# Filter norms as columns of 128 channels, spread by TensorE, and the filter spectra one turn later

## What is computed

```python
def hyena_filters(...):                       # weights only, no tokens
    h = (hid @ w3).reshape(L, ORDER, 2, D) * exp(-t * abs(deltas))
    h_fwd, h_bwd = h[:, :, 0], h[:, :, 1]
    two_sided = concatenate([h_fwd[:1] + h_bwd[:1], h_fwd[1:], zeros, flip(h_bwd[1:])])
    two_sided = two_sided * rsqrt(sum(square(two_sided), axis=0) + 1e-6)   # one norm per order and channel
    return rfft(two_sided, n=2 * L, axis=0)

def peer_ffn(h, ...):                         # 8 heads x 16 chosen experts for each token
    act = gelu(einsum('td,thkd->thk', t, u_tab[idx]))
    return einsum('thk,thkd->td', gate * act, v_tab[idx])
```

## Time and profile before

| | us |
|---|---|
| median of 3 runs | 1937.98 (1936.33 to 1944.38) |
| the profiled execution's own time | 1935.79 |
| its span in the trace | 1934.0 |
| TensorE matmul busy | 1690.3 (87%) |
| VectorE busy | 1500.2 (78%) |
| ScalarE busy | 593.4 (31%) |
| bytes moved | 665.11 MB, mean 344 GB/s |

### The profile page before, as it was taken

The page is one execution under the profiler, slowest core; times in us unless marked ns, Lnnn a source line. Parts: engine busy times, 40 slices in busy tenths (PEclk is TensorE's granted clock), DMA queues, the critical chain, the costliest instruction groups (busy, mean ns, idle before and its releaser), DMA issues.

```text
span 1934.0 us, 18185 instructions
## 1 busy us (share of the span) xinstructions
PE 1690.3 (87%) x5422; PEld 934.6 (48%) x5422; DVE 1500.2 (78%) x3548; ACT 593.4 (31%) x1427; POOL 483.3 (25%) x516
## 2 busy tenths in 40 slices
PE   5999999997999877899898999879989987877776
PEld 5778468653554432343343677545444433332232
DVE  6899996766778767888886699787678778777755
ACT  2555672312222323323242121023222232322221
POOL 0000000022334333343333100023333333333331
PEclk9999999998999998998999999889999999999999
DMA  8333118978999999999999775679999999999996
GB/s 348 120 120 113 50 58 316 387 276 347 364 427 419 426 408 406 380 418 413 425 414 426 312 302 201 245 294 415 427 426 426 421 425 414 417 426 420 426 417 280
DMA packets 95170, 665.11 MB, mean 344 GB/s; under 512 B 11323, under 2 KB 13020, under 8 KB 15456
## 3 DMA queue, kind: packets, MB, share of 16 engines
q0 software_dynamic: 73728, 536.90, 67.3%
q1 hardware_dynamic: 21344, 127.05, 17.0%
HBM read 662.79 MB, written 1.11 MB: 343 GB/s over the span
## 4 chain that ended last, share of the span: by engine, by line
PE 47%; DMA 24%; DVE 20%; issue 4%; ACT 2%; PEld 1%; DVEq 0%; PEldq 0%; POOL 0%; SPq 0%; POOLq 0%; ACTq 0%
DMA expert_rows<-in_p_uv,chosen_experts 23%; PE bank L1056 23%; DVE dot_products L2222 4%; PE bank L1032 4%; PE bank L818 3%; PE bank L862 3%; PE bank L934 2%; DVE conv_work_or_state L1860 2%; DVE silu_c_row_and_products L1668 2%; PE bank L878 1%; PE bank L889 1%; PE bank L1248 1%; PE bank L1092 1%; ACT weight_diagonal L1517 1%; PE bank L1175 1%
## 5 line engine op out<-in xcount | busy, mean ns | idle before, releaser
L1056 PE MATMUL bank<-expert_rows,weight_diagonal 128*128 128x512 f32 x2048 | 967.8, 617 | 173.5 <-ACT weight_diagonal L1517 172.8
L1288 POOL DMA_INDIRECT expert_rows<-in_p_uv,chosen_experts x512 | 483.1, 944 | 1424.3 <-PE bank L1056 795.1
L2222 DVE SCALAR_TENSOR_TENSOR dot_products<-expert_rows,bank 128x1024 f32<-128x1024 f32 x512 | 624.9, 1220 | 255.6 <-DMA expert_rows<-in_p_uv,chosen_experts 241.6
L1056 PEld LDWEIGHTS bank<-expert_rows,weight_diagonal 128*128 128x128 f32 x2048 | 385.2, 196 | 689.1 <-issue 398.0
L1517 ACT ACTIVATE weight_diagonal<-constants,expert_weights 128x128 f32<-128x128 f32 x512 | 177.8, 394 | 243.8 <-DVE expert_weights L2154 235.3
L1509 ACT ACTIVATE expert_gelu<-expert_dots 128x2 f32<-128x2 f32 x258 | 52.3, 203 | 627.4 <-DVE dot_products L2222 627.0
L818 PE MATMUL bank<-mixer_input_T_hi,weights_hi 128*128 128x512 f32 (+1 forms) x192 | 74.8, 389 | 22.0 <-DVE mixer_input_T_lo L1752 14.7
L1860 DVE SCALAR_TENSOR_TENSOR conv_work_or_state<-conv_work_or_state,channel_vectors 128x252 f32<-128x252 f32 (+1 forms) x192 | 82.5, 431 | 4.9 <-ACT conv_work_or_state L1371 0.4
L1175 PE MATMUL bank<-hyena_input_T,hyena_weight_block 128*128 128x256 f32 x320 | 71.1, 380 | 4.3 <-DMA hyena_weight_block<-in_h_in_blocks 4.3
L818 PE MATMUL bank<-mixer_input_T_lo,weights_hi 128*128 128x512 f32 (+1 forms) x192 | 72.4, 377 | 0.0
L818 PE MATMUL bank<-mixer_input_T_hi,weights_lo 128*128 128x512 f32 (+1 forms) x192 | 72.4, 377 | 0.0
(11 more groups left out here) (298 smaller groups left out, 1935.8 us busy)
## 6 DMA issues: line engine op xcount, KB each, us to landing
weight_block<-in_ada_rows SPq DMA_DIRECT2D x24, 1024.0 KB, 7.0
weight_block<-in_m_in_blocks SPq DMA_DIRECT2D x20, 1024.0 KB, 4.9
hyena_weight_block<-in_ada_rows SPq DMA_DIRECT2D x16, 1024.0 KB, 5.4
hyena_weight_block<-in_h_in_blocks SPq DMA_DIRECT2D x12, 1024.0 KB, 7.3
weight_block<-in_wq_blocks SPq DMA_DIRECT2D x11, 1024.0 KB, 7.6
expert_rows<-in_p_uv,chosen_experts POOLq DMA_INDIRECT x512
out_weights<-in_m_out_blocks SPq DMA_DIRECT2D x6, 1024.0 KB, 9.5
hyena_weight_block<-in_h_out_blocks SPq DMA_DIRECT2D x4, 1024.0 KB, 7.2
```

The costliest lines, as they stand in the source:

```text
L1056: last = mm(ps[b][:, :], dg[n % DIAG][:, :], uv[slot][:, D + h * 512:D + (h + 1) * 512], start=(r == 0 and k == 0), stop=end)
L1288: pool.indirect_dma_start(uv[slot][:, :], None, A[f"p_uv{l}"], bass.IndirectOffsetOnAxis(ap=chosen[:, s_, k:k + 1], axis=0)).then_inc(uv_l ...
L2222: stt(prod[:, :], uv[slot][:, 0:D], 1.0, rows_t, ALU.mult, ALU.mult, accum_out=dots[:, s_, k + j:k + j + 1]).then_inc(sem("dots_done"), 1)
```

## The change

The squares become the stationary operand and one column of the constants the moving one, so that the sum of a channel lands once, on the partition of that channel: 4 columns of 128 channels. Epsilon, root and reciprocal are taken on those 128x4 values. ScalarE then makes four diagonal matrices of them (`norm_diagonals`), TensorE multiplies these with a matrix of ones (`hrows`), which spreads the norms over all partitions again, and ScalarE copies the result to SBUF (`norm_rows`). In the second step the calls move: epsilon from k = 0 to k = 2, the root from 0 to 2, the reciprocal from 2 and 4 to 4, `hrows` stands at k = 7, the blocks of the spectrum go from k = 1, 3, 7, 9, 11 to 1, 8, 9, 11, 13, and their products from k = 6, 8, 10, 12, 14 to 8, 10, 12, 14, 14.

```diff
+    rsn_column = small[:, 1, 18:22]
+    rsn_diagonals = kT[:, 0:4, :]
...
                 plan.use(("hnorm", m), 4)
+                plan.use(("hrows", m), 4)
...
                     b = begin(("hnorm", m))
-                    for j, w in enumerate((FC_WS, FC_W1, FC_WD, FC_W1)):
-                        last = mm(ps[b][:, :], fc[:, w:w + P], sqr[:, j, :], start=(j == 0), stop=(j == 3))
+                    for c in range(4):
+                        for j, w in enumerate((FC_WS, FC_W1, FC_WD, FC_W1)):
+                            last = mm(ps[b][:, c:c + 1], sqr[:, j, c * P:(c + 1) * P], fc[:, w:w + 1], start=(j == 0), stop=(j == 3))
                     last.then_inc(full[b], 1)
-                elif second and k in (1, 3, 7, 9, 11):
-                    i = k // 2 if k < 4 else k // 2 - 1
+                elif second and k == 7:
+                    pe.wait_ge(sem("norm_diagonals"), m + 1)
+                    b = begin(("hrows", m))
+                    mm(ps[b][:, :], cst[:, C_ONE, :], rsn_diagonals.rearrange("p c k -> p (c k)"), start=True, stop=True).then_inc(full[b], 1)
+                elif second and k in (1, 8, 9, 11, 13):
+                    i = (1, 8, 9, 11, 13).index(k)
...
             def norm_root(m):
                 wait_read(act, ("hnorm", m))
-                f(rsn, rsn, ACT.Sqrt).then_inc(sem("norm_root"), 1)
+                f(rsn_column, rsn_column, ACT.Sqrt).then_inc(sem("norm_root"), 1)
+
+            def norm_diagonals(m):
+                act.wait_ge(sem("norm_reciprocal"), m + 1)
+                for c in range(4):
+                    last = f(rsn_diagonals[:, c, :], ident, ACT.Copy, scale=rsn_column[:, c:c + 1])
+                last.then_inc(sem("norm_diagonals"), 1)
+
+            def norm_rows(m):
+                if m:
+                    wait_read(act, ("hspec", m - 1, 4))
+                copy_out(("hrows", m), rsn, halves)
...
-                        if k == 0 and second:
-                            if m == 0:
-                                ln_root(l, 1, 0)
+                        if k == 0 and second and m == 0:
+                            ln_root(l, 1, 0)
+                        if k == 2 and second:
                             norm_root(m)
+                        if k == 4 and second:
+                            norm_diagonals(m)
+                        if k == 6 and second:
+                            norm_rows(m)
...
-                ts(rsn, halves(ps[b]), HY_EPS, None, ALU.add).then_inc(read[b], 1)
+                ts(rsn_column, ps[b][:, 0:4], HY_EPS, None, ALU.add).then_inc(read[b], 1)
...
-                after(step(V.reciprocal(rsn[:, i, :], rsn[:, i, :])))
+                V.reciprocal(rsn_column, rsn_column).then_inc(sem("norm_reciprocal"), 1)
...
             def filter_spectrum(m, i):
+                if i == 0:
+                    wait_read(dve, ("hrows", m))
...
-                elif second and k == 0:
+                elif second and k == 2:
                     filter_norm(m)
-                elif second and k in (2, 4):
-                    filter_reciprocal(m, k // 2 - 1)
-                if second and k >= 6 and k % PAIR == 0:
-                    filter_spectrum(m, (k - 6) // 2)
+                elif second and k == 4:
+                    filter_reciprocal(m)
+                elif second and k >= 8 and k % PAIR == 0:
+                    filter_spectrum(m, (k - 8) // 2)
+                    if k == 14:
+                        filter_spectrum(m, 4)
```

More of the change, by code:

```diff
@@ L2174, in filter_norm, with filter_reciprocal @@
                 b = wait_full(dve, ("hnorm", m))
-                ts(rsn, halves(ps[b]), HY_EPS, None, ALU.add).then_inc(read[b], 1)
-            def filter_reciprocal(m, i):
+                ts(rsn_column, ps[b][:, 0:4], HY_EPS, None, ALU.add).then_inc(read[b], 1)
+            def filter_reciprocal(m):
                 dve.wait_ge(sem("norm_root"), m + 1)
-                after(step(V.reciprocal(rsn[:, i, :], rsn[:, i, :])))
+                V.reciprocal(rsn_column, rsn_column).then_inc(sem("norm_reciprocal"), 1)
             def filter_spectrum(m, i):
                 h, o = divmod(m, 2)
+                if i == 0:
+                    wait_read(dve, ("hrows", m))
                 b = wait_full(dve, ("hspec", m, i))
```

## The result

The changed kernel takes 1946.22 us (median of 20 runs, 1939.04 to 1957.71), the kernel before 1935.68 in as many (1928.58 to 1944.38). The ratio is 1.0065, with a 95% interval of 1.0052 to 1.0078: slower by 0.65%, 12.6 us by the ratio and 10.5 by the medians. The forecast was +5.0 us, 1943, with an own range of 1940 to 1946, and no more than 0.5% from the kernel before. The sign was right, and the size was 40 to 50% of what came: 1946.22 lies just above the forecast's own range and inside the wider one (1936 to 1950). The profiled execution of the changed kernel took 1945.03 us with a span of 1943.2. Each is 9.2 more than that of the kernel before, and it is these 9.2 us that the trace can account for.

The account below looks back on a forecast made before the run. Gathers set the pace, TensorE next; behind the last gather TensorE ends the step. +5.3 at the end of step 15 and -0.3 in pieces 0 to 2 gave +5.0 us, 1943; own range 1940 to 1946, 8-in-10 range 1936 to 1950.

Parts of the forecast that it names:

- End of step 15, +5.3: Behind the last gathers: TensorE's and VectorE's delays make L1988 start at 1100.44 instead of 1095.09, +5.3 us.
- `hrows` 0.86: On TensorE behind unit 7: two more records, 0.86 us a piece.
- the hole behind it: TensorE idle 1.7 us a piece before unit 8, whose Gelu and diagonal queue behind ScalarE's copy, which waits for `hrows`.
- VectorE's wait on the last block: The last block stands behind unit 13; VectorE's product with it, ahead of unit 15's dot, waits for TensorE's backlog.
- the hole before the last unit: End of step 15: TensorE stands 1.5 us before unit 15 while VectorE's chain after the last block takes 3.2.
- The 0.64 us: Step 15: with a block gone, TensorE could start unit 6 at 1069.80, but its diagonal is usable at 1070.44.
- Pieces 0 to 2, -0.3 with bounds of 2: Second steps before the last piece: slots freed 2.6 us late, units 4 to 7 done 1.7 earlier; -0.3 us taken.
- a queue of 11.5 us: Gathers: one landed 11.53 us after issue, so slots freed a few us late cost nothing unless the queue runs dry.
- Squares, 3.5 us a piece: On TensorE: 32 one-column records at 0.11 us per load take 3.5 us, no change from 3.43; bounds 0 and 7.0.
- VectorE's relief, costed at nothing: VectorE gains 3.8 us a piece, 15 in all, worth nothing as TensorE has no gap; rival that it pays: 1923, chance 0.05.
- The clock as a rival: Holes of 1.5 to 1.7 us bring TensorE's clock down, 3.3 us once or twice: 1946 to 1950, up to 1955; chance 0.12.

Follow-up runs that it names:

- experiment 1: The changed kernel with 128 alike moving columns instead of one in the squares' matmuls; ratio to the kernel before 1.0027, 1938.9 us.
- experiment 5: The kernel before, its order and VectorE work kept, with only the one-column squares of the change; ratio 1.0027, 1938.99 us.
- experiment 7: The changed kernel with 128-column squares, `hrows` at k = 5 in bank 2, blocks at k = 1, 3, 9, 11, 12, products from k = 8; ratio 1.0007, 1936.33 us.
- experiment 4: The kernel before, norms on all partitions and no `hrows`, with every call at the place the change gives it; ratio 1.0012, 1936.5 us.
- experiment 6: The changed kernel with 128-column squares, `hrows` at k = 5 and the last product behind the next dots; ratio to the kernel before 1.0018, 1936.62 us.

## Why the prediction was right in its sign and half right in its size

- **End of step 15, +5.3: +5.4 measured.** Most of its parts came as worked out: `hrows` 0.86, the hole behind it (1.65 for 1.7, released by the diagonal with the copy just ahead), VectorE's wait on the last block, the hole before the last unit (1.22 for 1.5). One part came about otherwise. The 0.64 us for which TensorE should have stood before unit 6 are not in the changed kernel, since the lower clock behind the squares had made TensorE late already. So that clock costs the end little here, +5.4 for +4.9 in experiment 1, where TensorE does stand 0.33 us before unit 6. In experiment 5 the end is +2.9, but there the lower clock lasted twice as long behind the last squares. That the sum came to a tenth of a microsecond is luck: against the landing of unit 14 of step 14, unit 13 ended 1.9 us later than before, not 1.5, and from the end of the last block to the meeting it took 5.5 us, not 6.0.
- **Pieces 0 to 2, -0.3 with bounds of 2: +3.8.** This is the term that was mis-sized. The argument was that slots that come free 2.6 us late are covered by a queue of 11.5 us. For the holes and `hrows` it held: with both of them in place and the clock undisturbed the middle is at -0.3 (experiment 1). What was missing is a slow stretch in each piece on top: the 12 records behind the squares take 7.09 - 5.32 = 1.8 us more, half a step ahead of the new holes. With holes and `hrows` in place, the squares with one column cost the middle 4.1 us more than those with 128 (+3.8 for -0.3; 3.8 us by the last completion packets). The slow clock without the holes makes +1.4 or -0.5 (experiment 5, by the two readings). So it may be their sum against the depth of the queue that decides, of which I had only one; that is argued from single traces and not shown.
- **Squares, 3.5 us a piece: right.** 32 records in 3.5 us, 0.11 us each with its load, at one column as at 128. The Trainium skill (TensorE: Matmul & The Clock Gate, Back-to-back issue gap) has a floor of about 25 ns for a matmul taken alone, from which 0.8 us would be the estimate, and says that in a stream of load and matmul pairs both set the spacing; the trace agrees with the second. But I asked of the new form only how long it takes, and not what it does to the clock.
- **VectorE's relief, costed at nothing: right** as far as can be told. Experiment 7 keeps 14.7 us of it and is at 1.0007, and its interval begins at 0.9989.
- **The clock as a rival: right in kind, wrong in its trigger.** The prediction had it behind the new holes, at 0.12. Three stretches of the changed kernel with a hole of 1.48, 1.47 and 1.07 us in them, in the columns of the earlier trace rows:

```profile
834.50:844.50 10.00, 8.52 (x21) 3.62 (x20) 8.23 (x19) 2.28 (x7) 2.81 (x3) 1.00 1.01 426
1079.00:1089.00 10.00, 8.53 (x20) 3.53 (x19) 6.93 (x14) 2.87 (x10) 0.94 (x1) 1.00 1.01 427
1101.00:1104.00 3.00, 1.93 (x5) 0.68 (x4) 2.49 (x9) 2.09 (x4) 0.00 (x0) 1.00 0.99 418
```

  The granted clock is 1.00 in each. It fell instead behind squares through which TensorE never stood. The Trainium skill (TensorE: Matmul & The Clock Gate, What's actually happening) has the clock follow how busy TensorE was and idleness send it to the lower level. If busy is what the profile shows as busy, 3.50 of 3.50 us, the clock should have stayed up behind the squares, and experiment 5 does not agree with that.
- **The split of the 0.65%.** The one-column squares: 0.27 (experiment 5) to 0.38 (the changed kernel less experiment 1), each uncertain by 0.24. The rest, 0.27, is mostly the order, with the last block late and no block between the units 4 to 8: 0.12 by the ratio of experiment 4, whose interval reaches to nothing, and 4.5 us or 0.23 by its trace. For `hrows` with its copy that leaves 0.04 to 0.15, and experiment 7 has both at 0.07 in all, 0.25 by the upper end of its interval. None of these remainders is clear of noise. What experiment 7 shows is that the change's work can be had at about the time of before in other places.

It stays open why piece 1 of the first profile kept its clock, why the lower clock lasted 6.8 us behind some squares and 3.4 behind others, how `hrows` and the copy share what is left to them in time (no kernel had one without the other), how the slow stretch and the holes act together on the queue, and what makes the middle of experiment 6.

## What to carry to other kernels

When work on TensorE is reshaped, ask not only how long the new form takes but also what runs right behind it: matmuls of one column behind full weight loads cost nothing themselves and slowed the next 12 records by 1.8 us. Where the loads set the pace, as here, 128 moving columns cost no more than one, so a widened copy of the kernel is a cheap test. And two delays that a queue would cover one by one are better held against it together when they stand in the same few units, though no run here shows this apart from noise. Last, a single trace against a single trace can mislead: the same kernel had its lost transfers in other stretches the second time, and the lower clock lasted 3.4 us behind one of the squares and 6.8 behind another.

## What was not expected of the hardware

- After 32 one-column float32 records with 128x128 loads (3.50 of 3.50 us busy, at a granted clock of 0.93) the granted clock was 0.50 over the next 6.30 us (experiment 5, last squares); after the same number of 128-column records at the same pace it was 1.00 over 5.20 us (experiment 1).
- One column and 128 columns cost the same: 3.50 us for 32 records each.
- Holes of 1.07 to 1.48 us in TensorE's work left the granted clock at 1.00, where the earlier trace rows has 0.63 with one of 2.86. A hole of 2.86 us does not always bring it down. The changed kernel has one ahead of 888.27 with 1.00 behind it:

```profile
888.27 3.70 PE L1059 MATMUL bank<-expert_rows,weight_diagonal 128*128 128x512 f32 x8 [2.86 <-ACT weight_diagonal L1525]
888.20:892.20 4.00, 3.70 (x8) 1.44 (x8) 3.29 (x7) 2.59 (x7) 0.94 (x1) 1.00 1.03 399
```

  In the ten profiles, from 815 to 1103 us, none of the 70 holes of 0.95 to 1.91 us saw the lower clock begin in it or within 3.5 us behind it; of the 25 holes of 2.09 to 2.87 us 17 did.
